# Fourteen of 56 weight pairs in eight plain block products instead of seven Strassen-type ones, in one layer of a hybrid encoder

## The reference, cut to what matters

```
h  = RMSNorm(x);  u, v_g, q, k, v, g = split(h @ w_in)          # w_in: 1024 x 5632
A  = gelu(u) * (W_s * LayerNorm(gelu(v_g)) + b_s)               # in chunks of 128 tokens
B  = sliding-window attention of q, k, v (16 heads, 4 kv heads)
x  = x + (sigmoid(g_A) * (A @ w_pa) + sigmoid(g_B) * (B @ w_pb)) @ w_o
h2 = RMSNorm(x)
x  = x + (gelu(conv3(h2 @ w_up_gate)) * (h2 @ w_up_val)) @ w_down   # FFN width 2816
y  = RMSNorm_final(x), besides the new k, v, conv and v_g rows
```

## Time and profile before

| | |
|---|---|
| median of three runs | 1808.71 us |
| profiled execution | 1812.65 us, of it 1810.9 us span |
| TensorE matmul busy | 1659.8 us (92%) |
| VectorE, ScalarE, GpSimd busy | 1202.4, 692.3, 460.2 us |
| TensorE idle before line 1851 | 107.1 us |

### The profile page before, as it was taken

How to read it: one execution, slowest core, us unless ns; L and a number is a source line. 1 busy time by engine, 2 the same in 40 slices (tenths; PEclk the granted TensorE clock), 3 DMA queues, 4 the chain that set the end, 5 groups by cost and what they waited for, 6 DMA issues and landing times.

```text
span 1810.9 us, 31098 instructions
## 1 busy us (share of the span) xinstructions
PE 1659.8 (92%) x12278; PEld 1603.6 (89%) x12278; DVE 1202.4 (66%) x1950; ACT 692.3 (38%) x1276; POOL 460.2 (25%) x383
## 2 busy tenths in 40 slices
PE   4799999999999895968959879999999999999997
PEld 3699888888889895968949879999999999999997
DVE  6736565565646566649687777777777777666665
ACT  5434445454443324334334444333333333111112
POOL 3222121212123443233554522232222230000001
PEclk7899999999999998988979989999999999999999
DMA  7253434243435754442533322222222226222212
GB/s 234 76 172 114 126 90 128 88 133 92 121 103 162 221 155 171 155 175 91 152 109 113 119 59 72 72 85 72 72 88 79 72 72 256 79 80 95 96 72 100
DMA packets 240580, 209.39 MB, mean 116 GB/s; under 512 B 24759, under 2 KB 197619, under 8 KB 240435
## 3 DMA queue, kind: packets, MB, share of 16 engines
q1 hardware_dynamic: 240206, 207.32, 36.0%
q10 hardware_dynamic: 229, 0.08, 0.0%
HBM read 141.91 MB, written 65.45 MB: 115 GB/s over the span
## 4 chain that ended last, share of the span: by engine, by line
PE 62%; DVE 7%; issue 4%; DMA 4%; POOL 2%; ACT 2%; SPq 1%; DVEq 0%; ACTq 0%; POOLq 0%
PE ps L1851 43%; PE ps L2028 15%; DVE op_lo L1336 2%; DVE w_lo L1327 2%; PE ps L1926 1%; DMA quad<-m_spill 1%; DMA vg_t<-in_spill 1%; PE ps L1905 1%; DMA lo_f<-o_spill 1%; PE ps L1917 1%; PE ps L1951 1%; DMA gate_q<-in_spill 1%; POOL raw L876 1%; DVE lo_f L1362 1%; PE ps L1941 1%
## 5 line engine op out<-in xcount | busy, mean ns | idle before, releaser
L1851 PE MATMUL ps<-op_hi,w_hi 128*128 128x272 f32 x3136 | 674.4, 297 | 107.1 <-DVE quad L1437 33.0
L1851 PE MATMUL ps<-op_hi,w_lo 128*128 128x272 f32 x3136 | 657.3, 291 | 0.0
L1851 PE MATMUL ps<-op_lo,w_hi 128*128 128x272 f32 x3136 | 656.7, 291 | 0.0
L1851 PEld LDWEIGHTS ps<-op_hi,w_hi 128*128 128x128 f32 x3136 | 501.3, 192 | 136.0 <-issue 127.3
L1851 PEld LDWEIGHTS ps<-op_lo,w_hi 128*128 128x128 f32 x3136 | 502.6, 192 | 0.0
L1851 PEld LDWEIGHTS ps<-op_hi,w_lo 128*128 128x128 f32 x3136 | 499.0, 192 | 0.0
L1327 DVE TENSOR_TENSOR w_lo<-raw,w_hi 128x512 fp32r<-128x512 f32 x224 | 177.5, 813 | 173.2 <-ACT w_hi L1035 173.2
L865 POOL TENSOR_TENSOR w_f<-raw 128x512 f32<-128x512 f32 x56 | 83.8, 1497 | 667.6 <-PE ps L1851 635.6
L1765 DVE TENSOR_TENSOR xy<-ps,xy 128x728 f32<-128x728 f32 (+1 forms) x176 | 119.2, 719 | 95.0 <-PE ps L2028 95.0
L1035 ACT ACTIVATE w_hi<-raw 128x512 fp32r<-128x512 f32 x224 | 132.9, 624 | 126.9 <-PE ps L1851 99.6
L1327 DVE TENSOR_TENSOR w_lo<-w_f,w_hi 128x512 fp32r<-128x512 f32 x168 | 155.3, 950 | 18.5 <-ACT w_hi L1035 16.5
(11 more groups left out here) (166 smaller groups left out, 1830.9 us busy)
## 6 DMA issues: line engine op xcount, KB each, us to landing
in_spill<-quad SPq DMA_DIRECT2D x88, 272.0 KB, 2.1
raw<-in_w_in_dram SPq DMA_DIRECT2D x44, 512.0 KB, 5.2
raw<-in_w_up_dram SPq DMA_DIRECT2D x44, 512.0 KB, 4.6
g_spill<-value_out SPq DMA_DIRECT2D x22, 544.0 KB, 2.7
g_in<-g_spill SPq DMA_DIRECT2D x11, 1088.0 KB, 5.7
d_raw<-in_w_down_dram SPq DMA_DIRECT2D x22, 512.0 KB, 3.4
q_now<-in_spill SPq DMA_DIRECT2D x36, 128.0 KB, 2.4
gate_q<-in_spill SPq DMA_DIRECT2D x16, 272.0 KB, 5.2
```

The lines of the kernel that those rows point to most:

```text
L1851: last = pe.matmul(out[:, h, 0:HB], (w_hi, w_lo)[a][n][:, j, :], (op_hi, op_lo)[b][n][:, j, HB * h:HB * h + HB], start=FRESH[n] and j == 0 ...
```

## The change

Fourteen pairs (0, all of `PB`, `PA` and `OUT`, and 34) are made of the eight plain block products, and the other 42 stay at seven. A plain pair needs no sums of weights and no sums of its operand, no partial copies, and four weight blocks instead of seven. ScalarE copies each quadrant from PSUM (`quadrant_out`), in the output stage VectorE adds it to the residual (`residual_out`). The first four plain products use B11 and B21 only, the first half of the tokens. In pair 0 the first product may start when five tiles of x are scaled and seven are copied out; each tile has a buffer of its own, and the last tile's transposes and scales come between the first products. Operand sums stay for generations 0 and 4, and are made during pairs 0 and 34. `load_operands` moves one pair earlier, an attention step takes 9 ticks, the load of `vg_t` moves from 6 to 9 ticks before its transposes, and parts of the FFN norm and the first convolution step move into pair 35. The core of the diff:

```diff
+SEVEN = ((0, 0, 0, True), (1, 1, 1, True), (2, 2, 0, False), (3, 3, 2, True), (4, 4, 0, False), (5, 5, 1, True), (6, 6, 2, False))
+
+EIGHT = ((0, 0, 0, True), (4, 0, 1, True), (1, 1, 0, False), (5, 1, 1, False), (0, 7, 0, True), (4, 7, 2, True), (1, 6, 0, False),
+         (5, 6, 2, False))
+
+PLAIN = (0,) + tuple(range(PB, UP)) + (UP,)
...
+def slots(p):
+
+    return list(enumerate((0, 1, None, 2, 3, 4, 5, 6) if plain(p) else range(NPROD)))
...
+def order_of(p):
+
+    return (Q11, Q21, Q12, Q22) if plain(p) else (Q11, Q22, Q21, Q12)
...
-ATT0, ATT_STEP, NSTEP = 96, 10, KVH * NT
-LN0, LN_STEP = ATT0 + ATT_STEP * NSTEP + 17, 10
+ATT0, ATT_STEP, NSTEP = 96, 9, KVH * NT
+LN0, LN_STEP = ATT0 + ATT_STEP * NSTEP + 20, 10
...
+def summed(g):
+
+    return not all(plain(p) for p in range(FIRST_PAIR[g], END_PAIR[g]))
...
-        XT = 5
+        XT = 7
         xt = put(r_big, "xt", [P, XT, D])
-        xts = put(r_big, "xts", [P, 2, KT, P], at=XT * 4096)
+        xts = [put(r_op, f"xts{n}", [P, KT, P], at=4 * OP + 4096 * n) for n in range(4)] \
+            + [put(r_w, f"xts{4 + n}", [P, KT, P], at=at * WB) for n, at in enumerate((4, 6, 12))] \
+            + [put(r_tmp, "xts7", [P, KT, P]), put(r_big, "xts8", [P, KT, DEC], at=33792)]
         tab_rows = put(r_big, "tab_rows", [P, 2, P], at=28672)
...
-                m = ln_step(tick, -6)
+                m = ln_step(tick, -9)
...
+                    if p == FIRST_PAIR[g] - 2 and (n, j) == (0, 3):
+                        if g == 1:
+                            gated_all()
+                            for q in range(4):
+                                load_gate_b(PB, q)
+                        else:
+                            sp.wait_ge(s_op, OP_BASE[g])
+                        load_operands(g, src)
+                    if p == FIRST_PAIR[g] - 1 and (n, j) == (1, 0):
...
+                pool.wait_ge(s_op, op_count(g, 7))
                 if g == 0:
+                    pool.tensor_tensor(r12[:], r22[:], r12[:], ALU.subtract).then_inc(s_t3, 1)
...
+                if n == 6:
+                    weight_hi(0, 0)
+                    weight_hi(0, 4)
                     operand_hi(0, 0, "w")
                     operand_hi(0, 1, "w")
...
+            def quadrant_out(p, q):
+
+                n, region = {Q11: (2, 0), Q21: (3, 1), Q12: (6, 0), Q22: (7, 2)}[q]
+                act.wait_ge(s_product, product_count(p, n))
+                if p and q == Q11:
+                    act.wait_ge(s_comb, 4 * p)
+                free_place(p, q)
+                act.activation(two(destination(p, q)), reg[region][:, :, 0:HB], copy).then_inc(s_comb, 1)
...
+            weight_lo(0, 0)
+            operand_lo(0, 0, "w")
+            weight_lo(0, 4)
+            operand_lo(0, 1, "w")
+            weight_lo(0, 1)
+            for n in range(5, NT):
+                x_tile(n)
+                if n == 7:
+                    weight_lo(0, 5)
+            operand_lo(0, 7, "w")
             t_sum(0, 0, "w")
-            weight_lo(0, 0)
...
+            def residual_out(p, q):
+
+                n, region = {Q11: (2, 0), Q21: (3, 1), Q12: (6, 0), Q22: (7, 2)}[q]
+                dve.wait_ge(s_product, product_count(p, n))
+                if q == Q11:
+                    dve.wait_ge(s_comb, 4 * p)
+                dve.wait_ge(s_x_q[q], 16 * (p - OUT + 1))
+                out = two(out_quad(p, q)[:])
+                dve.tensor_tensor(out, out, reg[region][:, :, 0:HB], ALU.add).then_inc(s_comb, 1)
...
+                if (p, n, j) == (UP, 3, 1):
+                    mean_in()
+                if (p, n, j) == (UP + 1, 0, 0):
+                    factor_in(0)
+                if (p, n, j) == (UP + 1, 1, 0):
+                    factor_in(1)
...
+                if plain(p):
+                    if p == 0:
+                        if k < 2:
+                            pe.wait_ge(s_xts, 7 + k)
+                        if k == 5:
+                            pe.wait_ge(s_xts, NT)
+                    elif k == 0:
+                        if plain(p - 1):
+                            pe.wait_ge(s_comb, comb_count(p - 1, Q12))
+                        else:
+                            pe.wait_ge(s_copied, COPIES_BEFORE[p])
+                    elif k == 1:
+                        pe.wait_ge(s_comb, comb_count(p - 1, Q21))
+                    elif k == 5:
+                        pe.wait_ge(s_comb, 4 * p)
+                    if k == 4:
+                        pe.wait_ge(s_comb, comb_count(p, Q11))
+                    return
+                if k == 0:
...
+            def beside_first(k):
+
+                if k == 0:
+                    transpose_x(NT - 1)
+                if k == 1:
+                    spread_rstd(NT - 2)
+                if k == 2:
+                    spread_rstd(NT - 1)
...
```

More of the change, by code:

```diff
@@ new lines, in plain, with products @@
+def plain(p):
+    return p in PLAIN
+def products(p):
+    return EIGHT if plain(p) else SEVEN
+def slots(p):
+    return list(enumerate((0, 1, None, 2, 3, 4, 5, 6) if plain(p) else range(NPROD)))
+def order_of(p):
+    return (Q11, Q21, Q12, Q22) if plain(p) else (Q11, Q22, Q21, Q12)
+PRODUCTS_BEFORE = [sum(len(products(m)) for m in range(p)) for p in range(NPAIR + 1)]
+COPIES_BEFORE = [sum(0 if plain(m) else 3 for m in range(p)) for p in range(NPAIR + 1)]
+SUMS_BEFORE = [sum(0 if plain(m) else 4 for m in range(p)) for p in range(NPAIR + 1)]
@@ new lines, in product_count, with low_order, low_count, ahead @@
+def product_count(p, n):
+    return PRODUCTS_BEFORE[p] + n + 1
+LAST = PRODUCTS_BEFORE[NPAIR - 1]
+def low_order(p):
+    if plain(p):
+        return (0, 4, 1, 5) if p == 0 or plain(p - 1) else (0, 1, 4, 5)
+    return (3, 0, 4, 1, 2, 5, 6) if plain(p - 1) else (0, 1, 3, 2, 4, 5, 6)
+LOWS_BEFORE = [sum(len(low_order(m)) for m in range(p)) for p in range(NPAIR + 1)]
+def low_count(p, n):
+    return LOWS_BEFORE[p] + low_order(p).index(n) + 1
+def ahead(p, n, j, late):
+    if p + 1 == NPAIR:
+        return ()
+    if plain(p):
+        if plain(p + 1):
+            return {(5, 1): (0,), (6, 1): (4,), (7, 1): (1,)}.get((n, j), ())
+        return {(5, 1): (3,), (6, 0): (0,), (6, 3): (4,), (7, 1): (1,)}.get((n, j), ())
+    if plain(p + 1):
+        return {(3, 1): (0, 1), (5, 1 + 2 * late): (4,), (6, 1 + 2 * late): (5,)}.get((n, j), ())
+    return {(3, 1): (0, 1), (5, 1 + 2 * late): (3,), (6, late): (2, 4), (6, 3): (5,)}.get((n, j), ())
@@ L73, in key_rows @@
     return [P] if n == 0 else [P, P] if n < NT - 1 else [CACHE, DEC]
[L76 to L87, removed]
+FIRST_PAIR = (0, PB, PA, OUT, UP)
@@ L94, in generation, with op_place, t_count, place_freed @@
     return max(g for g in range(5) if FIRST_PAIR[g] <= p)
+def op_place(g, n):
+    return n if n < 7 else 4 if g else 2
 def op_count(g, n, part=None):
     return OP_BASE[g] + max(i + 1 for i, (m, q) in enumerate(OP_ORDER[g]) if m == n and part in (None, q))
+def t_count(g, i, part=None):
+    return T_BASE[g] + max(k + 1 for k, (m, q) in enumerate(T_ORDER[g]) if m == i and part in (None, q))
+def place_freed(p, n):
+    g = generation(p)
+    for k in reversed(range(len(products(p)))):
+        if op_place(g, products(p)[k][1]) == n:
+            return product_count(p, k)
+    return place_freed(p - 1, n)
@@ L102, in att_step, with weights_freed @@
+def weights_freed(p, n):
+    for k in reversed(range(len(products(p - 1)))):
+        if products(p - 1)[k][0] == n:
+            return product_count(p - 1, k)
+    return weights_freed(p - 1, n) if p > 1 else 0
 def att_step(tick, shift):
@@ L1206, in operands @@
             def operands(p, n, j):
[L1208 to L1218 removed]
+                todo = ()
@@ new lines, in product @@
+            def product(p, k, j):
+                if j == 0:
+                    product_waits(p, k)
+                place, operand, region, fresh = products(p)[k]
+                at, out = op_place(generation(p), operand), reg[region]
+                for i, (a, b) in enumerate(PASSES):
+                    for h in range(2):
+                        last = pe.matmul(out[:, h, 0:HB], (w_hi, w_lo)[a][place][:, j, :],
+                                         (op_hi, op_lo)[b][at][:, j, HB * h:HB * h + HB],
+                                         start=fresh and j == 0 and i == 0, stop=j == KP - 1 and i == 2,
+                                         skip_group_check=True)
+                if j == KP - 1:
+                    last.then_inc(s_product, 1)
@@ L1810, in _ @@
             pe.wait_ge(s_ident, 1)
-            for n in range(NT):
+            for n in range(8):
                 transpose_x(n)
```

741 lines of the change are left out of this document (377 added, 364 removed).

## The result

The changed kernel takes 1749.78 us (median of 4 runs, 1749.11 to 1750.18); the kernel before, on the same chip, 1810.13 us (1807.26 to 1813.73). The ratio is 0.9665, interval 0.9646 to 0.9684. The forecast was 1741, the range 1712 to 1776. The profiled span went from 1810.9 to 1747.3 us, 63.6 us less against 67.4 forecast.

The account below looks back on a forecast made before the run. TensorE, busy for 92% of the span, was taken as the bound. Terms 42.1 - 84.5 - 10 - 7 - 10 + 2 = -67.4 us on a span of 1810.9 gave 1743.5, and 1741 us for the median; range 1712 to 1776.

Parts of the forecast that it names:

- The bound and the price of a product: Whole kernel: TensorE bounds it; a product is 24 matmuls at 125.3 ns, 3.01 us; 14 added products cost +42.1 us.
- Changes of operand: Pairs 21 to 33, into PB, PA, OUT: losses of 46.5, 22.5, 23.5 us fall to 3, 3, 2; -84.5 us.
- the bound of -46 (half kept): Changes of operand, pairs 21 to 33: the smaller gain, half the loss kept if loads rather than sums set it.
- Gating and attention: Gating steps, pairs 16 to 20: earlier vg_t removes most waits, -10 us; attention at nine ticks loses a little, +2 us.
- rival D: Attention steps: at nine ticks each of 36 steps waits 1 us, the rest as forecast; 1775 us, chance 7%.
- The start: Pairs 0 and 1: first product near 31.5 us instead of 43.15, pair 2 near 103; -7 us without the added product.
- Into the FFN: Pairs 34 and 35: sums stay, made within pair 34 without slack; 6 us lost instead of 16.0, -10 us.
- The wait on `w_lo` in pair 35: Pair 35: a wait of some microseconds on w_lo, named as a sign that the forecast is right.
- A (all gaps close): Whole kernel: every term at its good end, -94 us, 1714 us; chance 18%.
- B: Changes of operand: half of their loss stays, gates waiting behind a burst of loads; -18 us, 1791 us, chance 15%.
- C's sign: Plain pairs: PE waits of 2 us and more on ScalarE's PSUM copies; rival slower, 1825 us at 3 us late, 4%.

Follow-up runs that it names:

- the table of four kernels: Four kernels, all with new attention and gating spacing: seven products, loads late 1800.9 us, early 1796.7; plain products, loads late 1766.1, early 1749.8.
- the run with the spacing alone: Kernel before, all pairs at seven products, loads unmoved; only attention steps at nine ticks and vg_t loads nine ticks ahead: 1800.93 us, ratio 0.9948.
- the late first product: Changed kernel with TensorE's last input transposes and spreads ahead of the first product, which waits for all tokens: 1745.27 us, ratio 0.9638.
- the reordering: Changed kernel with only the queue order of pairs 0 and 1 altered (ScalarE's block 3 and 4 splits later, VectorE's zeroing earlier): 1743.67 us, ratio 0.9630.
- the last kernel: Changed kernel with queues reordered, block 4's first sum on VectorE, last gate behind the split, input transposes between the first product's quarters: 1733.42 us, ratio 0.9577.
- the run with five plain pairs: Changed kernel with only the first pair of each stage plain (0, 22, 26, 30, 34), operand sums back: 1773.1 us, ratio 0.9798.

## Why the prediction was right, and where its sizes were off

- **The bound and the price of a product** held. A plain pair takes 24.0 us, a seven-product pair 21.0; fourteen added products cost 42 us.
- **Changes of operand** were the gain, as forecast, and a little larger into `PB` and `PA`: nothing stayed of the loss, where 3 us each had been kept. Into `OUT` 4.8 us stayed instead of 2, at a place that the forecast had taken as due: not a PSUM handover, but the last gate quadrant, whose load is 5.7 us late, in front of a split. Putting the gate behind the split won 3.3 of the 4.8 us. That sums and splits rather than loads set the loss is shown by the table of four kernels; the bound of -46 (half kept) was too far, since even with late loads pairs 21 to 25 kept only 14.6 us of it.
- **Gating and attention** gave 8.1 us for 8 forecast, and the run with the spacing alone isolates the term: its pairs 2 to 20 take 555.5 us, 7.4 less. The earlier `vg_t` is worth 8.7 of it (10 forecast), the denser attention costs 0.6 (2 forecast). TensorE's waits for `pt_sb` before the values rose from 2.1 us in five to 5.5 in eight; for `o_sb` before the scores, where rival D had put 36 us, it never waited.
- **The start** is the step that was mis-sized: -4 net, +0.7 measured. The first product came at 30.3 for 31.5, and the chain written out in the forecast held, with its dates 1 to 2 us off either way, up to its last link: the third product of pair 1 was put at 84 us and started at 84.5. But the end of the pair followed 23.8 us later, not 19. Five products are 15.1 us of that. I had not costed the value transposes there: they take 2.6 us and wait 4.1 us for `vt_in`, which SyncE asks for at 86.95 us, behind the store of pair 0's last quadrant (copied at 81.9) and two weight loads, and which lands 7.9 us later. After the wait TensorE goes at its lower clock of 1.2 GHz (granted 0.51 from 94.9 to 100.2 us), with two matmuls in 0.45 instead of 0.25 us. And I took tiles 7 and 8 waiting behind products as a given; the late first product shows that this was 4.3 us lost for nothing. The waits of 7.2 us for a copy and 4.2 us for `ws_t` were in no sum either; the reordering removed both, against a new one of 6.83 us.
- **Into the FFN** -3.4 instead of -7: 59.6 us less 398 matmuls of 125.3 ns leaves 9.7 us lost, not 6. Four waits of 0.9 to 3.1 us make 7.7 of it: 3.1 on a combined quadrant at the end of pair 35 and the others in the norm's statistics. The wait on `w_lo` in pair 35 that the forecast named as a sign did not come, so the sums and splits due before the third product of pair 35, from which the 6 us were worked out, are not where TensorE stood. No run isolated these waits, and in nine other traces with this stretch unchanged it takes 59.6 to 62.3 us.
- The rest of the difference lies outside the span. The forecast went from span to median with -2.5 us, from one execution of before; in the changed kernel the median is 2.5 us above the span. That is 5.0 of the 8.8 us by which 1741 missed 1749.8, and the terms are 3.8. That the terms came so close is partly luck: by stretches they miss by 10.8 us in one direction (start, `OUT`, FFN) and by 6.9 in the other.

Of the rivals, A (all gaps close) came true for two of the four changes of operand. B did not occur. C's sign, a wait of 2 us and more for a copy by ScalarE inside a plain pair, came once, 7.2 us in pair 0, and not in the other 27 handovers that it counted.

## What to carry to other kernels

A faster algorithm per block can lose to a plain one wherever its side work (sums, splits, partial copies) sits on engines that must deliver before the next block starts; count it per stage, and drop it for a whole stage, not for the first block. Transfers moved earlier pay only after the engine queue behind them is short. Starting the bound engine earlier can be worth little or nothing if its early work delays the chain that feeds it: put the feeding instructions between its pieces first, then look at the end of the stretch and not at its start.

## What the runs showed of the hardware

- VectorE and GpSimd, both with two operands in SBUF, hold one another up for whole instructions. GpSimd's sum, begun 0.04 us after VectorE's, took 7.06 us; less the 2.39 us until VectorE was done that is 4.67 us, so GpSimd's own price is below the 5.33 us that I had read as undisturbed; that sum began at 47.14 us, 0.58 us before a VectorE instruction ended at 47.72. GpSimd's 128x512 sum takes 1.27 us when VectorE is quiet (at 91.60 in the changed kernel) and 3.36 us (at 60.30) behind one of VectorE's; that one began at 59.11, while GpSimd's sum before it ran to 60.23, and took 3.39 us instead of 2.42. The Trainium skill ("SBUF — State Buffer", the shared port pair) describes such a lock; the trace agrees. So a sum moved *to* the busier VectorE could shorten the chain: the median fell by 4.7 us.
- Waits of TensorE mostly go with a lower clock after them: the mean granted clock was 0.84 in pairs 0 and 1 with waits of 7.2, 4.2 and 4.1 us in them, and 0.94 in the same pairs of the last kernel, with 5.2 and 2.3 us left. Not each wait costs it: behind 4.1 us for `vt_in` it was 0.51 for 5.3 us, and behind 3.6 us at the same place of the run with five plain pairs 1.00; in pairs 21 to 25 it went from 0.89 to 1.00.
